# 128 of 512 tokens leave the dense expert layers: VectorE multiplies their fetched rows

## What is computed

```python
q = (xi @ w_q).reshape(n, 8, 2, 128)
s = einsum('nhpc,hpkc->nhpk', q, sub_keys)            # 128 scores on each of two sides
ts, ti = lax.top_k(s, 16)                              # best 16 of each side
cand_s = ts[:, :, 0, :, None] + ts[:, :, 1, None, :]   # 256 pairs
best_s, best_p = lax.top_k(cand_s, 16)                 # best 16 pairs: idx = i * 128 + j
gate = softmax(best_s)
act = gelu(einsum('nd,nhkd->nhk', xi, u[idx]))
out = einsum('nhk,nhkd->nd', gate * act, v[idx])
```

## Time and profile before

| | us |
|---|---|
| three runs | 2975.09, 2980.21, 2984.22 |
| median | 2980.21 |
| the profiled execution | 2981.47 |
| its span in the trace | 2980.2 |
| PE busy | 2732.6 |
| DVE busy | 1594.7 |
| POOL busy | 1173.3 |
| ACT busy | 1005.9 |

### The profile page before, as it was taken

One profiled execution on the slowest core, in us unless ns is written; L12 is line 12 of the kernel. 1 busy time (PEld: TensorE's weight loads), 2 busy tenths in 40 slices (PEclk: granted clock), 3 DMA queues, 4 the chain that ended last, 5 costly groups with the idle time before them and its releaser, 6 DMA issues.

```text
span 2980.2 us, 34358 instructions
## 1 busy us (share of the span) xinstructions
PE 2732.6 (92%) x13413; PEld 1409.3 (47%) x13606; DVE 1594.7 (54%) x3589; ACT 1005.9 (34%) x1145; POOL 1173.3 (39%) x942
## 2 busy tenths in 40 slices
PE   6998599968999979999999999999998988989998
PEld 4455367634444444444444444444444456534443
DVE  2046532222799999999815656556536356243101
ACT  3126532323332244544432232322324234244310
POOL 4223253423334323323346656556532510244630
PEclk8989567789999989999999999999999999899999
DMA  4212022221354445566567565656621110113320
GB/s 154 85 57 85 31 85 85 93 91 57 115 168 127 152 142 180 192 212 212 201 194 258 194 218 187 216 199 196 216 104 57 57 60 19 57 57 113 116 82 29
DMA packets 174609, 384.20 MB, mean 129 GB/s; under 512 B 6709, under 2 KB 73315, under 8 KB 167920
## 3 DMA queue, kind: packets, MB, share of 16 engines
q1 hardware_dynamic: 171584, 368.20, 36.3%
q0 software_dynamic: 2864, 13.79, 1.3%
HBM read 312.77 MB, written 69.21 MB: 128 GB/s over the span
## 4 chain that ended last, share of the span: by engine, by line
PE 64%; DVE 28%; ACT 3%; POOL 2%; issue 2%; DMA 1%; ACTq 0%; DVEq 0%; POOLq 0%
PE psum L427 17%; PE psum L428 17%; PE psum L426 17%; DVE gated_one_hot_b L1794 5%; DVE gated_one_hot_b L1796 5%; DVE one_hot_a L1792 4%; PE psum L674 3%; POOL weight_low L1956 2%; PE psum L656 2%; PE psum L481 2%; PE psum L895 1%; PE psum L568 1%; DVE pair_scores L1757 1%; DVE norm_value L1474 1%; PE psum L569 1%
## 5 line engine op out<-in xcount | busy, mean ns | idle before, releaser
L1956 POOL TENSOR_TENSOR weight_low<-weight_stage,weight_high 128x512 bf16<-128x512 f32 (+1 forms) x885 | 1132.8, 1314 | 1453.0 <-ACT weight_high L982 1453.0
L427 PE MATMUL psum<-x_low,weight_high 128*128 128x512 bf16 (+2 forms) x1832 | 692.9, 378 | 35.8 <-DMA sub_keys<-sub_keys_dram 21.0
L426 PE MATMUL psum<-x_high,weight_high 128*128 128x512 bf16 (+2 forms) x1793 | 676.7, 377 | 24.7 <-DVE x_low L1480 9.2
L428 PE MATMUL psum<-x_high,weight_low 128*128 128x512 bf16 (+2 forms) x1832 | 691.6, 377 | 1.4 <-issue 0.2
L982 ACT ACTIVATE weight_high<-weight_stage 128x4096 bf16<-128x4096 f32 (+2 forms) x112 | 399.3, 3568 | 523.1 <-PE psum L428 510.7
L426 PE MATMUL psum<-hidden_high,weight_high 128*128 128x512 bf16 x1004 | 380.5, 379 | 1.1
L428 PE MATMUL psum<-hidden_high,weight_low 128*128 128x512 bf16 x1003 | 380.1, 379 | 1.1
L427 PE MATMUL psum<-hidden_low,weight_high 128*128 128x512 bf16 x1003 | 380.1, 379 | 1.1
L1811 DVE TENSOR_TENSOR hidden_low<-expert_act,hidden_high 128x512 bf16<-128x512 f32 x128 | 183.6, 1492 | 260.2 <-ACT hidden_high L1274 260.2
L426 PEld LDWEIGHTS psum<-x_high,weight_high 128*128 128x128 bf16 (+1 forms) x1856 | 184.3, 99 | 271.8 <-issue 35.8
L428 PEld LDWEIGHTS psum<-x_high,weight_low 128*128 128x128 bf16 (+1 forms) x1856 | 184.9, 100 | 212.3 <-issue 12.6
(11 more groups left out here) (289 smaller groups left out, 2975.4 us busy)
## 6 DMA issues: line engine op xcount, KB each, us to landing
weight_stage<-peer_u_dram SPq DMA_DIRECT2D x32, 2048.0 KB, 9.9
weight_stage<-peer_v_dram SPq DMA_DIRECT2D x32, 2048.0 KB, 8.1
act_dram<-norm_value SPq DMA_DIRECT2D x128, 256.0 KB, 10.1
gate_dram<-gate_matrices SPq DMA_DIRECT2D x16, 2048.0 KB, 14.7
gates<-gate_dram SPq DMA_DIRECT2D x32, 1024.0 KB, 11.8
expert_act<-act_dram SPq DMA_DIRECT2D x32, 1024.0 KB, 14.0
weight_stage<-mlp_w_dram SPq DMA_DIRECT2D x16, 2048.0 KB, 8.2
weight_stage<-ada_w_dram SPq DMA_DIRECT2D x12, 2048.0 KB, 7.9
```

The source lines that it names most:

```text
L426: self.nc.tensor.matmul(out, left[0], right[0], start=first, stop=False)
L427: self.nc.tensor.matmul(out, left[0], right[1], start=False, stop=False)
L428: return self.nc.tensor.matmul(out, left[1], right[0], start=False, stop=last)
L1956: ins = nc.gpsimd.tensor_tensor(m.w_low[:, n % SPLITS, at], m.w_stage[:, n % STAGES, at], m.w_high[:, n % SPLITS, at], ALU.subtract)
```

## The change

The tokens are divided. The first 384 (`DT`) go through the dense way as before. The last 128, one token to a partition (`ROW_TILE`), are routed first and then handled by rows: POOL fetches for pick x of head h the 128 rows of `u` (one to a token, 512 KB) by an indirect DMA into one of four slots (`ask`); DVE multiplies the slot by the tokens' activations and sums along the row ("dot"); ACT applies gelu to a head's 16 sums (`row_experts`); DVE adds `v`'s rows, fetched in the same way, times the weight to `row_sum` ("sum"). There are 128 dots and 128 sums, 256 uses in all. PE turns `row_sum` and adds it to the last columns of the banks in the last group. The uses are dealt out by tables: 24 in each of the other three routing tiles, three in every two one-hot steps, 4 ahead of the groups, and 4 in each of groups 0 to 26. POOL asks for rows behind the split of a weight block.

All dense matmuls and tiles have 384 columns in place of 512. The fill tables are new: 4 tiles, then 32, 24 and 24 up to each set of picks, two tiles in three one-hot steps (48 steps of 8 tokens), 12 at the end. A one-hot step is four two-input bf16 instructions of 1024 elements: compare a, compare b, and two multiplications by the gate's parts. The wait for the sub-keys is behind the first query tile, and `iota_keys` is loaded ahead of the queries. The split of the weights into high and low parts is as before, POOL's eight pieces too.

```diff
-OC = 16
+OC, OI = 8, 4
+ROW_TILE, DT = QT - 1, SEQ - P
+ROW_SLOTS = 4
...
 # TensorProgram.columns_tile
         for t in range(KT):
+            if rows is not None:
+                self.normed_rows(t, rows)
...
+    def normed_rows(self, t, banks):
+        nc.tensor.wait_ge(*s.normed.at("ln2", t))
+        nc.tensor.transpose(k.psum[:, banks[t // 4], P * (t % 4):P * (t % 4 + 1)], m.norm2.value[:, t % 4, DT:SEQ],
+                            m.ident[:, :]).then_inc(*s.turned.up("normed_rows", t))
...
 # fill: slice(0, SEQ) -> slice(0, DT); TensorProgram.route
-        nc.tensor.wait_ge(*s.in_sub_keys.at())
+            if hp == 0:
+                nc.tensor.wait_ge(*s.in_sub_keys.at())
...
 # TensorProgram.experts
-                    ins = self.three_products(k.bank(sums[t]), (high[:, b, cols], low[:, b, cols]),
+                    ins = self.three_products(k.bank(sums[t], DT), (high[:, b, cols], low[:, b, cols]),
...
+                if n == NG - 1:
+                    if t == 0:
+                        nc.tensor.wait_ge(*s.row_used.at(len(ROW_USES) - 1))
+                    ins = nc.tensor.transpose(k.psum[:, sums[t], DT:SEQ], m.row_sum[:, P * t:P * (t + 1)], m.ident[:, :])
...
-for _t, _n in enumerate((10, 14, 14, 14)):
...
+ROUTE_TILES = [ROW_TILE] + list(range(ROW_TILE))
+ROUTE_FILL = [(range(0, 4), None), (None, ROW_TILE, "gates")]
+_at = 4
+for _t, _end in zip(ROUTE_TILES[1:], (36, 60, 84)):
+    ROUTE_FILL += [(range(_at, _end - 5), None), (None, _t, "gates"), (range(_end - 5, _end), None), (None, _t, "picks")]
+    _at = _end
+HOT_STEPS = DT // OC
+HOT_FILL = [range(_at + 2 * _n // 3, _at + 2 * (_n + 1) // 3) for _n in range(HOT_STEPS)]
...
+ROW_USES = [("dot", _h, _k) for _h in range(2) for _k in range(TOPK)]
+for _h in range(2, PH):
+    for _k in range(TOPK):
+        ROW_USES += [("dot", _h, _k), ("sum", _h - 2, _k)]
+ROW_USES += [("sum", _h, _k) for _h in (PH - 2, PH - 1) for _k in range(TOPK)]
+ROWS_ROUTE = [3 * PH * _o for _o in range(QT)]
+ROWS_HOT = [ROWS_ROUTE[-1] + 3 * (_n + 1) // 2 for _n in range(HOT_STEPS)]
+ROWS_LAST = ROWS_HOT[-1] + 4
+ROWS_GROUP = [min(len(ROW_USES), ROWS_LAST + 4 * (_n + 1)) for _n in range(NG)]
+def rows_asked(g):
+    tile, marks = EG * g, [(0, 0), (12, 0), (28, ROWS_ROUTE[1]), (52, ROWS_ROUTE[2]), (76, ROWS_ROUTE[3] + 3),
+                           (110, ROWS_HOT[-1]), (NK, ROWS_LAST)]
+    for (a, x), (b, y) in zip(marks, marks[1:]):
+        if a <= tile < b:
+            return 0 if tile < 12 else x + (y - x) * (tile - a) // (b - a) + ROW_SLOTS
...
 # VectorProgram
+    def rows(self, until):
+        while self.used < until:
+            nc.vector.wait_ge(*s.in_rows[i % ROW_SLOTS].at(i))
+            if kind == "dot":
+                nc.vector.scalar_tensor_tensor(row, row, 1.0, m.hn_rows[:, :], ALU.mult, ALU.mult,
+                                               accum_out=m.row_dot[:, at]).then_inc(*s.row_used.up(i))
...
+                    nc.vector.scalar_tensor_tensor(m.row_sum[:, :], row, m.row_weight[:, at], m.row_sum[:, :], ALU.mult,
+                                                   ALU.add).then_inc(*s.row_used.up(i))
...
 # VectorProgram.route, behind each top16 of tiles 0 to 2
+                    self.rows(ROWS_ROUTE[o - 1] + hp + 1)
...
 # VectorProgram.gate_matrices
-            for x in range(OC):
-                nc.vector.tensor_scalar(m.left[:, v, x, :], m.iota[:, :], number_a, None, ALU.is_equal)
-                nc.vector.tensor_scalar(m.gated[0][:, v, x, :], m.iota[:, :], number_b, gate, ALU.is_equal, ALU.mult)
-                nc.vector.tensor_scalar(m.gated[1][:, v, x, :], m.iota[:, :], number_b, gate_low, ALU.is_equal, ALU.mult)
+            nc.vector.tensor_tensor(m.left[:, v], iota, number_a, ALU.is_equal).then_inc(*s.step.up())
+            if n >= 1:
+                nc.vector.wait_ge(*s.hot.at(n - 1))
+            nc.vector.tensor_tensor(m.right[:, :, :, :], iota, number_b, ALU.is_equal).then_inc(*s.step.up())
+            nc.vector.wait_ge(*s.step.now())
+            nc.vector.tensor_tensor(m.gated[0][:, v], m.right[:, :, :, :], gate_high, ALU.mult).then_inc(*s.step.up())
+            nc.vector.tensor_tensor(m.gated[1][:, v], m.right[:, :, :, :], gate_low, ALU.mult).then_inc(*s.hot.up(n))
+            self.rows(ROWS_HOT[n])
...
 # VectorProgram.experts
+        self.rows(ROWS_LAST)
         for n in range(NG):
...
+            self.rows(ROWS_GROUP[n] - 2)
             for b in range(EG):
                 nc.vector.wait_ge(*s.hid_high.at(n, b))
...
+            self.rows(ROWS_GROUP[n])
...
 # PoolProgram.run and fill
         for n in range(NG):
             self.begin(("v", n))
+            self.ask(ROWS_GROUP[n])
...
+                self.ask(rows_asked(tile // EG))
+    def ask(self, until):
+        while self.asked < until:
+            if i == 0:
+                nc.gpsimd.wait_ge(*s.routed.at("row_lists"))
+            if i >= ROW_SLOTS:
+                nc.gpsimd.wait_ge(*s.row_used.at(i - ROW_SLOTS))
+            index = bass.IndirectOffsetOnAxis(ap=m.row_index[:, layer, pick:pick + 1], axis=0)
+            nc.gpsimd.indirect_dma_start(m.rows[i % ROW_SLOTS], None, v if layer else u, index).then_inc(
+                *s.in_rows[i % ROW_SLOTS].up(i))
```

More of the change, by code:

```diff
@@ L741, in route @@
             chosen, what = chosen
-            if what == "gates":
+            if what == "gates" or chosen == ROW_TILE:
                 continue
@@ L1205, in linear_attention, with row_experts @@
             self.head_norm("gla_head", GLA_HEADS - 1, part)
+    def row_experts(self, used):
+        nc, s, m = self.nc, self.s, self.m
+        while self.row_heads < PH and LAST_DOT[self.row_heads] < used:
+            h = self.row_heads
+            at = slice(TOPK * h, TOPK * (h + 1))
+            nc.scalar.wait_ge(*s.row_used.at(LAST_DOT[h]))
+            nc.scalar.activation(m.row_act[:, at], m.row_dot[:, at], ACT.Gelu).then_inc(*s.row_act.up(h))
+            self.row_heads += 1
     def fill(self, tiles):
@@ L1215, in fill @@
                 nc.scalar.wait_ge(*s.act_spilled[tile % 4].at(tile - 4))
-            nc.scalar.activation(m.norm2.value[:, tile % 4, :], k.tile_bank(event), ACT.Gelu).then_inc(
+            nc.scalar.activation(m.norm2.value[:, tile % 4, 0:DT], k.tile_bank(event, DT), ACT.Gelu).then_inc(
                 *s.activated.up(*event))
@@ L1772, in route @@
                                     ALU.mult).then_inc(*s.routed.up("picks", t))
+            if t == ROW_TILE:
+                self.row_lists()
+                continue
             at = slice(P * t, P * (t + 1))
             nc.vector.wait_ge(*s.copied.at("picks", t))
-            nc.vector.tensor_copy(m.gate_high[:, :], m.pick_t[:, 2, at]).then_inc(*step.up())
-            nc.vector.wait_ge(*step.now())
-            nc.vector.tensor_tensor(m.pick_t[:, 3, at], m.pick_t[:, 2, at], m.gate_high[:, :], ALU.subtract).then_inc(
-                *s.routed.up("split", t))
+            nc.vector.tensor_tensor(m.pick_b[:, 3, at], k.psum[:, k.bank_of["picks", t], 2 * P:3 * P],
+                                    m.pick_b[:, 2, at], ALU.subtract).then_inc(*s.routed.up("split", t))
@@ L1780, in gate_matrices @@
     def gate_matrices(self):
         nc, s, m = self.nc, self.s, self.m
+        hots = [P, OC // OI, NK, OI]
         nc.vector.wait_ge(*s.in_iota_keys.at())
-        nc.vector.wait_ge(*s.routed.at("split", QT - 1))
-        nc.vector.tensor_copy(m.iota[:, :], m.iota32[:, :]).then_inc(*s.step.up())
+        nc.vector.wait_ge(*s.routed.at("split", ROUTE_TILES[-1]))
+        nc.vector.tensor_copy(m.iota[:, :, :], m.iota32[:, :].unsqueeze(2).to_broadcast([P, NK, OI])).then_inc(
+            *s.step.up())
@@ L2014, in run @@
                 self.fill(stretch)
-        nc.gpsimd.wait_ge(*s.routed.at("split", QT - 1))
-        nc.gpsimd.dma_start(m.iota32[:, :], d["iota_keys"]).then_inc(*s.in_iota_keys.up())
-        for n in range(SEQ // OC):
+        for n in range(HOT_STEPS):
             self.fill(HOT_FILL[n])
```

158 lines of the change are left out of this document (110 added, 48 removed).

## The result

| | us, median (range) |
|---|---|
| kernel before | 2980.43 (2975.09 to 2984.22) |
| kernel after | 3113.99 (3112.13 to 3121.26) |
| ratio | 1.0454, 95% interval 1.0431 to 1.0477 |

The change makes the kernel 134 us slower. The forecast was 2910, with a range up to 3025: wrong in sign and outside the range.

The account below looks back on a forecast made before the run. PE was taken to set the groups' end, with DVE's order deciding in routing and one-hots; DVE and POOL would take PE's place. Terms -7 + 134 - 142 - 15 - 40 = -70 gave 2910 us, range 2790 to 3025.

Parts of the forecast that it names:

- Queries: Query stage: the first query tile runs in PE's wait for the sub-keys, -7 us (0 to -10).
- Routing: Routing: 72 row uses at 1.75 us on DVE, landing and late rows; +138, with `iota_keys` +134 (+85 to +200).
- PE will be covered: Routing: PE needs 312 us behind the first four tiles, less than DVE's 3 x 122.
- One-hots: One-hot stage: batched bf16 instructions at twice float32's pace, 48 steps of 5.95 us, 286 against 428: -142 us.
- Last fills: Last 12 fill tiles: each falls from 5.18 to 3.90 us, -15 us.
- Groups: Expert groups: a chain of rounding, split, asks, landing, use and remainder gives 20.2 us a group, 623 against 663: -40.
- The bound of 24.3 a group: Groups: the slow end of the estimate, 24.3 us a group, +71 us.
- GpSimd's ask as the pace: Slow rival: POOL's queue of asks between splits sets the pace from about 2.8 us an ask; 3070, chance 0.13.
- one-hots without the double rate: Slow rival, one-hot stage: 1.46 us an instruction, 403 us in place of 286; 3027, chance 0.10.
- The couplings do not bite: Fast rival: routing +100, one-hots -178, groups at 17 us (-126); 2755 at best, about 2800, chance 0.23.
- Landings of 8 us and rows late in the routing: No-change rival: full queues make groups 21.4 us (+34), late rows cost the routing +35; 2979, chance 0.08.
- the two slow rivals: Whole kernel: POOL's ask sets the pace (3070, chance 0.13); batched one-hots not twice as fast (3027, chance 0.10).

Follow-up runs that it names:

- uses alone: Kernel after with VectorE's 256 row uses kept but no row fetched, the buffers filled with zeros once: 2763.5 us, ratio 0.9280.
- Spread asks: Kernel after with asks spread between the eight pieces of a split, in the routing up to hidden tile 84 and in the groups: 2950.66 us, ratio 0.9908.
- ask-first kernel: Kernel after, but in the groups POOL asks for group n's rows before it splits block n+1: 2962.8 us, ratio 0.9947.
- fetches alone: Kernel after with all 256 row fetches but no use of them on VectorE, the sum being zeros: 2715.3 us, ratio 0.9106.

## Why the prediction was wrong

**Queries (-7).** The first query copy came 14.1 us after the first x_high, where before has 23.2, so the wait for the sub-keys left the path, and 5.8 us were left at the last query. They did not reach the picks: the row tile's compares met GpSimd's pieces, which fell earlier in before (by line, median 796 ns against 418; before's line is L1752, 408/418/1374).

```profile
L1882 DVE TENSOR_TENSOR pair_scores<-best_rank,iota_picks x16: 416/796/1375, 793.7 to 816.3; 128x256 f32<-128x256 f32 x16
```

**Routing (forecast +138 between the picks, measured +203).** The price of the uses was right, on the high side, for a kernel without fetches: uses alone give 340 - 230 = 110, and the sum had 126 for them. The failed term is the fetches': 5 us for the first landing and 9 for late rows and further pieces. The runs show 93 us in its place (433 - 340): beside uses alone the 72 uses take 194 us for 109, 13 of them held behind a whole run of pieces where the forecast had half a piece, VectorE waits 28 us for rows, and its other instructions take 18 less. Spread asks gave 40 of the 93 back. The forecast also had GpSimd's waits for used rows cost nothing "as long as DVE is a slot ahead". They are 166 us in the routing, and behind them PE waits for the low parts of blocks, 77 us where it waits 5.7 with uses alone:

```profile
PE psum L445 <- POOL weight_low L2097: 77.1, 14, 12.6
POOL rows_a L2217 <- DVE rows_a L1811: 76.0, 24, 11.8
```

One more thing was not seen: without any row the stage still takes 273 us, as some 70 tiles of hidden values now stand there (24 a tile for 14) and PE is busy 273 of 273. "PE will be covered" held only as long as VectorE was slower.

**One-hots (-142, measured -110).** The instruction was right (0.685 for 0.67 without meetings). With uses alone the stage takes 265 us, less than the forecast 286; 53 us come with the fetches. That PE's matmuls would take 0.08 us longer each was not considered at all: "16 small matmuls (1.2) and 2.6 of tile: covered" took before's duration for a new layout. Beside the rows it did not decide; alone it turned the part into a loss.

**Last fills (-15, measured -11).** Right within 4 us.

**Groups (-40, measured +59).** The mechanism was the forecast's, link by link; two sizes were off. The chain took 26.5 us for 24.1: two uses stand in it, not one, and the landing came 8.2 us after the first ask began where the sum had 2.4 + 5.5 for two asks and a landing, while the split was shorter (9.0 for 10.4). And the group behind the pause takes 20.4 us, not 15.6, because PE's granted clock is 0.78 there; I had taken 0.95 from the one-hots, where PE's pauses are short. The sum had the chain 1.2 us a group too short, and 0.3 for the clock, which costs 2.4: the clock is the larger part of the miss. Over 27 groups, (46.9 - 40.4) / 2 = 3.3 us each are 88 of the 99 us of error (27 x 23.5 + 5 x 15.6 = 712 of the measured 722). The bound of 24.3 a group was named (+71), and 23.5 came; in the total I had let it fall below the tenth that was left out.

**The rivals.** GpSimd's ask as the pace (0.95 us) and one-hots without the double rate both fell. "The couplings do not bite" (2755 to 2800) is what the kernel with uses alone shows, 2764: a good price for a kernel without the coupling. "Landings of 8 us and rows late in the routing" was nearest, and got 0.08 and a price of 2979: it charged 35 us over the forecast for the routing and 34 for the groups, where 65 and 99 came, and 32 in the one-hots. Each coupling was priced as a delay of its own, with a bound of its own; in all three stages they share one ring of four buffers and the same two queues, and they came together. That is also why the range was too short. Its upper end does not fit the chances either: the two slow rivals, priced at 3070 and 3027, hold 0.23 above 3025, and the text says that a tenth is left out.

By the Trainium skill (SBUF — State Buffer, section Who interferes with whom) two SBUF inputs on VectorE and a GpSimd read exclude each other, and issue order decides who blocks. The turns of 1.57 us agree. A hold over eight pieces in a row goes beyond it, as the section speaks of one instruction. What the holds cost in time is another matter: taking 345 us of them out of the ask-first kernel gave 11 us.

## What to carry to other kernels

When a new helper path runs on two in-order engines that wait on each other, price the ring: walk one buffer through ask, landing, use and next ask, with all that stands before each of them in its engine's queue. Here uses alone cost 120 us, fetches alone 72 and both 470, and moving one ask ahead of one split gave 151 back. A pause of PE costs twice, once for itself and once for the slow clock behind it; and when a layout is changed for one engine's rate, look at how the next engine reads it.

## What the runs showed of the hardware

- An indirect fetch of 128 rows of 4 KB occupies GpSimd for 0.95 us (median of 256), 0.4 more than the direct transfer of the earlier trace rows, and its row was usable about 8 us after the ask began when a block load of 2 MB started beside it.
- After 10.8 us without work TensorE ran a group of 96 matmuls at a granted clock of 0.78, in 20.4 us for 15.6, a mixture of its two levels (1.2 and 2.4 GHz); with pauses of 1.9 us it was 0.97.
- A 128x128 bf16 matmul whose operands are every fourth value takes 0.297 us, with neighbouring values 0.219.
- A bf16 product or compare of 1024 elements with two inputs takes 0.69 us on VectorE, also when one input is repeated along an outer direction, and 1.22 when one input is repeated along the innermost direction.
- VectorE instructions with two SBUF inputs took turns with GpSimd's pieces in kernels without indirect fetches, and were held for whole runs of eight pieces (up to 10.7 us) in kernels with them.
